# Prompt attention by pairs of heads: two heads side by side on TensorE, the mask added by a matmul, one pass over the scores

## What is computed

```python
SEQ, HEAD_DIM, SB_HEADS, SB_BLOCK = 1024, 64, 8, 128     # the prompt
DEC_BATCH, DEC_SEQ, PAST_LEN, PAGE_SIZE = 8, 8, 8192, 128  # the samples, K/V in pages

def stick_breaking_attention(q, k, v, bias):
    for qs in range(0, Lq, blk):
        ke = off + qs + blk
        z = einsum("bqhd,bkhd->bhqk", q[:, qs:qs + blk], k[:, :ke]) / sqrt(d) + bias_f
        causal = arange(ke)[None, :] < qpos[:, None]
        log_1mb = where(causal, log_sigmoid(-z), 0.0)
        later = cumsum(log_1mb, axis=3, reverse=True) - log_1mb
        w = where(causal, exp(log_sigmoid(z) + later), 0.0)
        outs.append(einsum("bhqk,bkhd->bqhd", w, v[:, :ke]))
```

## Time and profile before

| | us |
|---|---|
| median of 3 runs | 5064.89 |
| the 3 runs | 5061.01 to 5067.65 |
| the profiled execution's own time | 5062.52 |
| its span, first to last instruction | 5060.7 |

### The profile page before, as it was taken

The page is one execution under the profiler, slowest core; times in us unless marked ns, Lnnn a source line. Parts: engine busy times, 40 slices in busy tenths (PEclk is TensorE's granted clock), DMA queues, the critical chain, the costliest instruction groups (busy, mean ns, idle before and its releaser), DMA issues. The chain is left out here.

```text
span 5060.7 us, 66242 instructions
## 1 busy us (share of the span) xinstructions
PE 4144.9 (82%) x25213; PEld 3234.3 (64%) x25213; DVE 2347.5 (46%) x3820; ACT 1101.2 (22%) x2197; POOL 907.8 (18%) x832
## 2 busy tenths in 40 slices
PE   7978788887377879999997857564699777999996
PEld 7845566665377438989895445454245636988985
DVE  1189766665799333443435323223302525344345
ACT  1155555554000012111110202020001202111110
POOL 0034211111376021111112030311000102101112
PEclk9977799999688889999997868675798588999998
DMA  2110399998000201111111031324110111111111
GB/s 78 61 38 1 153 408 406 405 404 326 8 1 1 78 17 42 50 37 46 41 42 36 5 113 39 137 72 141 34 34 1 36 42 34 42 50 33 50 41 52
DMA packets 207058, 459.62 MB, mean 91 GB/s; under 512 B 28805, under 2 KB 113645, under 8 KB 203710
## 3 DMA queue, kind: packets, MB, share of 16 engines
q1 hardware_dynamic: 206814, 456.36, 24.7%
HBM read 440.87 MB, written 15.44 MB: 90 GB/s over the span
## 5 line engine op out<-in xcount | busy, mean ns | idle before, releaser
L1575 DVE TENSOR_TENSOR x<-x,f_d 128x512 f32<-128x512 f32 (+1 forms) x576 | 393.2, 687 | 348.6 <-PE f_d L1481 345.4
L1481 PE MATMUL f_u<-xH,f_w1h 128*128 128x364 f32 (+1 forms) x1536 | 508.4, 331 | 22.9 <-DVE f_w1l L1567 22.9
L1481 PE MATMUL f_u<-xL,f_w1h 128*128 128x364 f32 (+1 forms) x1536 | 508.1, 331 | 0.0
L1481 PE MATMUL f_u<-xH,f_w1l 128*128 128x364 f32 (+1 forms) x1536 | 507.9, 331 | 0.0
L1481 PE MATMUL f_d<-f_w2h,f_hh 128*128 128x512 f32 x1152 | 457.7, 397 | 8.8 <-DVE f_w2l L1567 8.8
L1481 PE MATMUL f_d<-f_w2h,f_hl 128*128 128x512 f32 x1152 | 457.3, 397 | 0.0
L1481 PE MATMUL f_d<-f_w2l,f_hh 128*128 128x512 f32 x1152 | 457.2, 397 | 0.0
L1554 POOL TENSOR_TENSOR f_hl<-f_h,f_hh 128x364 fp32r<-128x364 f32 (+1 forms) x192 | 184.1, 966 | 1329.2 <-ACT f_hh L1543 1329.2
L1591 DVE TENSOR_TENSOR f_h<-f_h 128x364 f32<-128x364 f32 (+1 forms) x192 | 103.1, 538 | 555.7 <-ACT f_h L1537 555.7
L1481 PEld LDWEIGHTS f_u<-xH,f_w1h 128*128 128x128 f32 x1536 | 291.8, 190 | 25.0 <-issue 23.8
L1481 PEld LDWEIGHTS f_u<-xL,f_w1h 128*128 128x128 f32 x1536 | 291.8, 190 | 1.3
(11 more groups left out here) (423 smaller groups left out, 7513.8 us busy)
## 6 DMA issues: line engine op xcount, KB each, us to landing
ss_kv<-in_cache_sb_kv SPq DMA_DIRECT2D x336, 512.0 KB, 8.3
x<-in_cache_sb_kv SPq DMA_DIRECT2D x176, 512.0 KB, 8.0
w<-in_ffn_w SPq DMA_DIRECT2D x64, 1024.0 KB, 5.5
ds_qb<-ds_q SPq DMA_DIRECT2D x24, 1024.0 KB, 6.3
ds_kc<-in_cache_dil_kv SPq DMA_DIRECT2D x16, 1024.0 KB, 7.8
x<-in_x_prompt SPq DMA_DIRECT2D x16, 512.0 KB, 6.5
pe_raw<-in_w_in_even SPq DMA_DIRECT2D x8, 1024.0 KB, 5.9
ds_kc<-in_cache_dil_kv SPq DMA_DIRECT2D x16, 512.0 KB, 5.8
```

The lines of the kernel that those rows point to most:

```text
L1481: mm = pe.matmul(out, a, b, start=(n == 0), stop=(n == len(parts) - 1))
L1575: v.tensor_tensor(K.x[0:r, t, cs], K.x[0:r, t, cs], dn_b[(c * DOWN + u) % 4][0:r, :], ALU.add).then_inc(added, 1)
```

## The change

The unit of work becomes a pair of heads, c, and a query block: 32 steps. Each of the two PSUM score buffers belongs to one head of the pair. TensorE issues the scores of the two heads alternately, from partitions 0 to 63 and 64 to 127, and their values alternately into output partitions 0 to 63 and 64 to 127. The causal mask of the last block is added to the scores in PSUM by a matmul with the identity, so the mask product and the mask addition go. The queries are scaled by 1/8 as they are copied out of the projection. One pass of VectorE takes the scores: z = min(score + bias, 40), and l is made from z; the maximum goes. Every other copy of turned weights moves from ScalarE to VectorE. The weights overwrite z. The buffers are five z, four l, four wT. The orders are new: TensorE has the turn of the even unit of pair s-2, the scores of pair s, the turn of the odd unit of pair s-2, the values of pair s-3. In the paged stage the single pass and the missing maximum are the same.

```diff
 # project_even: copies of qT carry the scale
-                    run(SLABS[s][1][:, 2 * SLABS[s][2] + f, n0:n0 + nn], banks[i % 8][:, 0:nn])
+                    scaled = HD ** -0.5 if dst_is_q(s) else None
+                    run(SLABS[s][1][:, 2 * SLABS[s][2] + f, n0:n0 + nn], banks[i % 8][:, 0:nn], scaled)
 # stick_prompt
+    steps = [(c, qb) for c in range(SBH // 2) for qb in [*range(0, NB, 2), *reversed(range(1, NB, 2))]]
+    ZS, LS, TS = 5, 4, 4
-                sp.dma_start(masks[:, 0, :], io["c_strict"]).then_inc(loaded, 16)
-                sp.dma_start(masks[:, 1, :], io["c_strict_neg"]).then_inc(loaded, 16)
+                sp.dma_start(hide[:, :], io["c_strict_neg"]).then_inc(loaded, 16)
 # TensorE
+                def scores(p):
+                    if p >= 1:
+                        pe.wait_ge(taken, 2 * p)
                     for n in range(0, ke, 512):
                         m = min(512, ke - n)
+                        for hh in range(2):
+                            lo = HD * hh
+                            pe.matmul(zp[hh][:, n:n + m], T["qT"][lo:lo + HD, c, qb * P:(qb + 1) * P],
+                                      T["kT"][lo:lo + HD, c, n:n + m], start=True, stop=(n + m < ke))
+                    for hh in range(2):
+                        mm = pe.matmul(zp[hh][:, ke - P:ke], K.ident[:, :], hide[:, :], start=False, stop=True)
                     mm.then_inc(logits, 1)
                 def turn_weights(u):
                     pe.wait_ge(weights, u + 1)
                     if u >= 1:
-                        pe.wait_ge(wT_ready, u)
+                        pe.wait_ge(wT_ready[(u - 1) % 2], (u - 1) // 2 + 1)
+                pe.wait_ge(loaded, 32)
+                for s in range(NSP + 3):
+                    if 0 <= s - 2 < NSP:
+                        turn_weights(2 * (s - 2))
+                    if s < NSP:
+                        scores(s)
+                    if 0 <= s - 2 < NSP:
+                        turn_weights(2 * (s - 2) + 1)
+                    if 0 <= s - 3:
+                        values(s - 3)
 # VectorE
+                    v.wait_ge(logits, u // 2 + 1)
+                    if u >= ZS:
+                        v.wait_ge(turned, u - ZS + 1)
+                    v.tensor_scalar(z[:, u % ZS, 0:ke], zp[u % 2][:, 0:ke], bias[:, h:h + 1], ZCAP, ALU.add, ALU.min).then_inc(taken, 1)
+                for s in range(NSP + 4):
+                    for hh in range(2):
+                        if s < NSP:
+                            take_scores(2 * s + hh)
+                    for hh in range(2):
+                        if 0 <= s - 1 < NSP:
+                            sum_later(2 * (s - 1) + hh)
+                    if 0 <= s - 2 < NSP:
+                        copy_weights(2 * (s - 2) + 1)
+                    if 0 <= s - 4:
+                        keep_output(s - 4)
 # GpSimd, one subtraction for a unit
+                    g.tensor_tensor(z[:, u % ZS, 0:ke], z[:, u % ZS, 0:ke], l[:, u % LS, 0:ke], ALU.subtract).then_inc(arg, 1)
 # ScalarE
+                for s in range(NSP + 2):
+                    if 0 <= s - 2:
+                        copy_weights(2 * (s - 2))
+                    for part in (exponentials, logarithms):
+                        for hh in range(2):
+                            if s < NSP:
+                                part(2 * s + hh)
+                    for hh in range(2):
+                        if 0 <= s - 1 < NSP:
+                            take_weights(2 * (s - 1) + hh)
 # stick_sample, each group; the same before the loop
-                    v.tensor_scalar(z[:, g % 3, :], zb[g % 2][:, 0:2 * PAGE], HD ** -0.5, bias[:, 0:1], ALU.mult, ALU.add)
-                    v.tensor_scalar(l[:, g % 3, :], zb[g % 2][:, 0:2 * PAGE], cap[:, 0:1], None, ALU.min).then_inc(S["z_ready"], 1)
+                    v.tensor_scalar(z[:, g % 3, :], zb[g % 2][:, 0:2 * PAGE], bias[:, 0:1], ZCAP, ALU.add, ALU.min).then_inc(S["z_ready"], 1)
-                    step(v.tensor_tensor(l[:, g % 3, :], z[:, g % 3, :], l[:, g % 3, :], ALU.max))
```

More of the change, by code:

```diff
@@ L400, in stick_prompt @@
         op = [ctx.enter_context(nc.psum_tensor(f"sp_op{i}", [P, 512], F32)) for i in range(2)]
[L401 to L404, removed]
+        loaded, ones_set, logits, taken, exp1, log1p, summed, arg, weights, turned, out_done, out_copied, kept = (
+            K.sem("sp_" + n) for n in ("ld", "ones", "lg", "z", "e1", "ln", "sum", "arg", "w", "trn", "od", "oc", "kept"))
+        wT_ready = [K.sem("sp_wTa"), K.sem("sp_wTv")]
+        keys = lambda u: (steps[u // 2][1] + 1) * P
         with nc.Block() as block:
@@ L459, in _ @@
                 v.wait_ge(ones_set, 1)
-                v.wait_ge(loaded, 48)
-                step(v.tensor_scalar(cap[:, :], bias[:, :], -HD ** 0.5, ZCAP * HD ** 0.5, ALU.mult, ALU.add))
+                v.wait_ge(loaded, 32)
                 v.tensor_copy(T["qTs"][:, :, :], T["qT"][:, :, SEQ:NT]).then_inc(kept, 1)
@@ L468, in take_scores @@
                 def take_scores(u):
-                    h, qb = units[u]
-                    ke = (qb + 1) * P
-                    v.wait_ge(logits, u + 1)
-                    if u >= 3:
-                        v.wait_ge(weights, u - 2)
-                    v.tensor_scalar(z[:, u % 3, 0:ke], zp[u % 2][:, 0:ke], HD ** -0.5, bias[:, h:h + 1], ALU.mult, ALU.add)
-                    if u >= 3:
-                        v.wait_ge(arg, u - 2)
-                    v.tensor_scalar(l[:, u % 3, 0:ke], zp[u % 2][:, 0:ke], cap[:, h:h + 1], None, ALU.min).then_inc(z_ready, 1)
+                    h, ke = 2 * steps[u // 2][0] + u % 2, keys(u)
@@ new lines, in exponentials, with logarithms @@
+                def exponentials(u):
+                    ke = keys(u)
+                    a.wait_ge(taken, u + 1)
+                    if u >= LS:
+                        a.wait_ge(arg, u - LS + 1)
+                    a.activation(l[:, u % LS, 0:ke], z[:, u % ZS, 0:ke], ACT.Exp).then_inc(exp1, 1)
+                def logarithms(u):
+                    ke = keys(u)
+                    a.wait_ge(exp1, u + 1)
+                    a.activation(l[:, u % LS, 0:ke], l[:, u % LS, 0:ke], ACT.Ln, bias=ones[:, :]).then_inc(log1p, 1)
@@ L612, in stick_sample @@
         qbd = sb("qbd", [P, DB, 4, QUAD])
[L613 removed]
+        ones, carry0 = sb("ones", [P, 1]), sb("carry0", [P, 4])
         zn, ln_, wnT = sb("zn", [P, 4, NSMP]), sb("ln", [P, 4, NSMP]), sb("wnT", [NSMP, 4, P])
```

133 lines of the change are left out of this document (51 added, 82 removed).

## The result

The change makes the kernel slower by 0.37%. The median is 5081.64 us (7 runs, 5075.09 to 5085.63), that of the kernel before 5064.89 on the same chip; the ratio is 1.0037, 95% interval 1.0027 to 1.0047. The forecast was 5053 us, range 5015 to 5080. The profiled execution took 5081.97 us with a span of 5080.1, against 5062.52 and 5060.7.

What follows compares the result with a forecast made beforehand. A closed chain across engines bounds the prompt stage: 44.0 us outside TensorE plus 30.4 on it per group, stage 305.5 against 312.6; with 2.5 from the paged stage, 9.6 off 5062.5 gives 5053 us, range 5015 to 5080.

Steps and rivals of the forecast that it cites:

- The chain: Prompt stage loop: take of second head, scan, subtraction, weight exponential, turn, scores, mask, next take; 74.4 us for eight steps.
- rival 3: Prompt stage: the loop doesn't close and VectorE stays the bound, stage 188 us, total 4935 us; chance 0.05.
- Rival 4: Prompt stage TensorE: the two heads' matmuls run one after the other, 48 us more, 5101 us; chance 0.05.
- my prices: TensorE costs in the chain: 36 blocks and 8 steps take 19.8 us at 2.4 GHz, 36.3 us at 1.2 GHz.
- G: GpSimd's subtraction in the prompt stage, 11.24 us for eight widths, taken from the earlier kernel's lines.
- the 0.7 us a group: TensorE's part of the prompt chain: old value work delays the narrow steps, 0.7 us in each group.
- Rival 2: Prompt stage: turn, scores and mask at 1.2 GHz in all steps, stage 337.5 us, total 5085 us; chance 0.18.
- the other arms: Prompt loop: ScalarE's passes where width rises, 0.96 plus 0.6 us, and turn buffer waits where it falls, 0.7 us, per group.
- Entry: Start of the prompt stage, where the mask must land before the first scores: 5.4 us.
- The drain behind the last take: End of the prompt stage: two widths of scan and subtraction, weight exponential, turn, copy, values; 8.8 us.
- The drain rule: Mask matmuls on TensorE: each change of tiling mode drains it, 0.15 us a step, 4.8 us over the prompt stage.
- The paged stage: Stage after the prompt stage: head and tail get shorter, steady part unchanged, 2.5 us less, between 0.9 and 4.

Runs made afterwards that it cites:

- run 2: The changed kernel with TensorE issuing the scores of pair s ahead of the turn of pair s-2: 4980.76 us, ratio 0.9835.
- run 9: The changed kernel with the scan's broadcast ones in PSUM instead of SBUF, one output bank, output copy first in VectorE's step: 5046.91 us, ratio 0.9968.
- run 7: The changed kernel with the second scan waiting for the first head's subtraction and 87 extra matmuls a group filling TensorE's gaps: 5037.3 us, ratio 0.9944.
- run 6: The changed kernel without the two mask matmuls of a pair, causal mask left out: 5055.4 us, ratio 0.9981.
- run 3: The kernel before with only the changed kernel's paged stage and scaled query copies, its prompt stage keeping order and two passes: 5061.22 us, ratio 0.9995.

## Why the prediction was wrong

**Right: what stops being the bound.** VectorE left it. Its share fell to 0.48 (forecast 0.57; its weight copies were cheaper, 23.5 us against 26, and the scans overlap their neighbours), the stage became no shorter for it, and VectorE waits 5.2 us a step for scores (about 4). The chain is the one I wrote down, link by link, so rival 3 (4935 us) falls for this kernel. But "I find no buffer that opens it" looked at buffers only; the list's order does (run 2).

**Right: the two heads overlap.** Rival 4 falls. In the changed kernel's timeline the scores of two heads over 640 keys take 1.40 us at a granted clock of 0.92, where my prices at the high level give 5 x 0.228 + 0.22 = 1.36, and those over 1024 keys 3.79 at 0.50, where they give 8 x 0.45 + 0.28 = 3.88:

```profile
434.71 1.40 PE L433 MATMUL sp_zp<-kT,qT 64*128 64x512 f32 x8
...
455.34 3.79 PE L433 MATMUL sp_zp<-kT,qT 64*128 64x512 f32 x8
```

**Wrong, the step that decided: the subtraction's price.** I took G = 11.24 us for eight widths from the earlier trace rows into a place where it has another neighbour; there it was 18.9 (75.7 / 4). In the chain it was 72.5 us over 30 steps; with nothing in its way it is 43.0 (run 9). That is 29.5 us, more than the 26.5 by which the stage missed its forecast (332.0 against 305.5). The trace of before had the conflict, with another victim. Its timeline, in rows that the prediction left out:

```profile
317.31 1.07 DVE L483 TENSOR_TENSOR sp_l<-sp_z,sp_l 128x896 f32<-128x896 f32 x1
...
322.98 1.22 DVE L483 TENSOR_TENSOR sp_l<-sp_z,sp_l 128x1024 f32<-128x1024 f32 x1
323.00 1.51 POOL L510 TENSOR_TENSOR sp_z<-sp_z,sp_masks 128x128 f32<-128x128 f32 x1
...
327.07 2.35 POOL L509 TENSOR_TENSOR sp_z<-sp_z,sp_l 128x1024 f32<-128x1024 f32 x1 [2.55 <-DVE sp_l L485]
...
328.67 1.56 DVE L483 TENSOR_TENSOR sp_l<-sp_z,sp_l 128x768 f32<-128x768 f32 x1
```

A maximum over 768 keys took 1.56 us beside a subtraction that had started before it, and one over 896 keys took 1.07 by itself; GpSimd's mask addition over 128 keys took 1.51 us behind a maximum that had started 0.02 us earlier. The subtraction itself was never the victim, since a scan of before is followed by an output copy and two takes, which read PSUM. The new order has scan behind scan. The prediction named the sign ("if GpSimd's subtraction changes its price without VectorE's maximum beside it") and gave it no price and no rival of its own.

**Mis-sized: TensorE in the chain.** These 30 steps turn 138 blocks and score 140. My prices give 75.5 us for them all at the high and 138.8 all at the low level, and the forecast had 117 (two thirds of the way, with the 0.7 us a group). Measured 124.6, so some 7 us more. With the short subtraction of run 9 it is 118.9: most of these 7 us follow from the subtraction too, which is in the gaps in front of TensorE's work. I had written the gaps of the wide steps (640, 896, 1024 and 768 keys, by what VectorE takes) as about 4, 5, 6 and 5 us; they were about 4, 6.3, 7.9 and 7.5, and with the short subtraction of run 9 about 3.4, 5.4, 6.3 and 5.7. The step that I priced worst is a narrow one, that of 512 keys. Behind a gap of 4.7 us, which I had not listed, its turn, scores and mask took 3.85 us on average, where my low price is 3.72. So the narrow steps came out 58% of the way from high to low, where I had 30, and the wide ones 85%, where I had 78. The prices themselves held: with the gaps filled and the subtraction short (run 7) the steps of 768, 896 and 1024 keys take 2.74, 3.32 and 3.12 us, and my prices at the high level give 2.73, 3.32 and 3.08. And I misread the gap of 3.26 us in the earlier trace rows as standing before the low level. It stood behind the fall. TensorE had been idle for 1.98 us until 315.11 and worked without a pause from there to 317.64, and within that work the granted clock went from 1.00 to 0.50 (windows view of the kernel before):

```profile
316.00:317.00 1.00, 1.00 (x3) 0.52 (x4) 1.00 (x2) 0.00 (x0) 0.90 (x2) 1.00 0.00 0
317.25:317.50 0.25, 0.25 (x2) 0.00 (x0) 0.25 (x2) 0.08 (x1) 0.00 (x0) 0.50 0.00 0
```

The stage's mean clock, 0.73, missed the 0.65 to 0.7 that I named: it is a mean over all of the stage, and the chain's own TensorE work stands right behind the gaps. Rival 2 (all low, 5085 us) names nearly the right time and only part of the cause: it would have had to bring 139 us.

**Too high: the rest.** From the first take of the stage to the last the forecast had 291.3 us, the trace 315.7, 24.4 more. Of these the two terms above are +29.5 and +7, so that -12 is in the others: the other arms, for which I had 2.3 us a group, 9.2 in all, hardly appear (the hop in front of the weight exponential is 3.2 us in 30 steps, 3.8 with the short subtraction, the wait before the turn 1.6), and back-to-back VectorE instructions overlap by more than I gave them, about 5 us over scans and second takes. Without the lock the same kernel is at 5046.9 us (run 9), so with the right price for the subtraction these errors would have left me too high by 6 us, inside the range.

**Entry and drain.** Entry 4.8 us (5.4), or 5.3 from the changed stage's own first instruction at 260.4. Nothing was seen of the projection's scale: VectorE's copies into qT took 534 ns in the mean, 535 before. The drain behind the last take was 11.5 us (8.8), which has two subtractions in it.

**The drain rule.** I weighed 4.8 us for the mask's switch of tiling mode. Mask and switch together cost 26 us in the chain (run 6), between my prices at the two levels, 18.7 and 34.9 us (32 x (0.435 + 0.15) and 32 x (0.86 + 0.23)); the switch by itself stays unmeasured.

**The paged stage.** -4.5 us here and -3.4 in run 3, against -2.5 (0.9 to 4): once just beyond the range and once inside it, and too small to count.

## What to carry to other kernels

Before a duration is carried over from a trace, look at what runs on the other engine at both its old and its new place: between a VectorE instruction with two SBUF operands and a GpSimd instruction over SBUF the one that starts second paid here, inside its own busy time, so that no wait is shown. Where a loop closes on itself, ask of each engine's list whether the instruction that others wait for could stand ahead of one that waits itself; here that one move was worth 101 us where the whole change lost 17. And where TensorE's work behind a gap is on the chain, look at its clock: filling the gaps with work that nobody reads gave 25 us back.

## What the runs showed of the hardware

- A VectorE scan with a broadcast operand in SBUF and a GpSimd subtraction over SBUF exclude each other for the whole length of the first (3.70 us instead of 2.08, or 3.20 instead of 2.01). With that operand in PSUM they run side by side at full speed (88.6 us instead of 119.6 for 64 subtractions), and the scan costs no more.
- Useless matmuls can pay: up to 87 more in each of four groups raised the clock of the stage from 0.73 to 0.89 and saved 25 us.
